# Routing of the sample tokens with two weight pieces kept in their buffers and a third buffer laid over keys and values

## The reference

```python
y = concat(attention_out, gdn_out) @ w_out              # mixer projection, 1024 x 1024
h = h + y
xb = rmsnorm(h, norm2)
q = (xb @ wq).reshape(-1, HP, 2, DPK // 2)              # HP = 8 heads; wq is 1024 x 2048
s = einsum('thcd,hcnd->thcn', q, keys)                  # 128 keys for each half of each head
s1, i1 = top_k(s[:, :, 0], 16);  s2, i2 = top_k(s[:, :, 1], 16)
cand = s1[..., :, None] + s2[..., None, :]              # 256 sums, of which the best 16
e = ...                                                 # number of an expert, 16384 in all
gate = softmax(sc);  hid = einsum('td,thkd->thk', xb, u[e])
h = h + einsum('thk,thkd->td', gate * gelu(hid), v[e])
```

## Time and profile before

| | |
|---|---|
| median of 3 runs | 2113.99 us |
| the profiled execution | 2111.61 us, span 2109.9 us |
| PE, DVE, ACT, POOL busy | 81%, 63%, 38%, 37% of the span |
| bytes moved | 779.61 MB; 369 GB/s over the span |
| chain that ended last | PE 36%, DMA 32%, DVE 16%, ACT 7% |
| L948, gathers | 576 issues |
| L782, loads of `w_route` | 20 issues of 2304 KB |
| L780, loads of `w_mixer` | 10 issues of 2048 KB |

### The profile page before, as it was taken

How to read it: one execution, slowest core, us unless ns; L and a number is a source line. 1 busy time by engine, 2 the same in 40 slices (tenths; PEclk the granted TensorE clock), 3 DMA queues, 4 the chain that set the end, 5 groups by cost and what they waited for, 6 DMA issues and landing times.

```text
span 2109.9 us, 20560 instructions
## 1 busy us (share of the span) xinstructions
PE 1713.4 (81%) x6211; PEld 863.1 (41%) x6211; DVE 1333.7 (63%) x3023; ACT 801.0 (38%) x2371; POOL 778.8 (37%) x704
## 2 busy tenths in 40 slices
PE   5889799988897878889797879978895567776877
PEld 1333364547453445445344535443551223442211
DVE  1343514344797657887665888865787866669554
ACT  1342321231545523563533455453243332323433
POOL 3123010111344543436334444634433554444442
PEclk9889899999999999999898999999898879888999
DMA  9999633128899999999999999999999999999997
GB/s 331 325 348 340 223 116 112 48 100 325 354 426 415 427 428 428 426 419 413 426 407 427 427 426 403 419 414 426 427 426 411 427 428 427 428 426 427 427 427 318
DMA packets 137479, 779.61 MB, mean 369 GB/s; under 512 B 14863, under 2 KB 23839, under 8 KB 59784
## 3 DMA queue, kind: packets, MB, share of 16 engines
q0 software_dynamic: 88384, 621.30, 70.6%
q1 hardware_dynamic: 45504, 149.69, 18.9%
q10 hardware_dynamic: 3480, 7.31, 0.9%
HBM read 762.27 MB, written 16.26 MB: 369 GB/s over the span
## 4 chain that ended last, share of the span: by engine, by line
PE 36%; DMA 32%; DVE 16%; ACT 7%; issue 4%; POOL 2%; SPq 1%; POOLq 1%; ACTq 0%; another core or an unknown queue 0%; DVEq 0%
DMA sb_uv<-in_peer_uv,sb_eidx 28%; PE bank L2145 17%; DVE sb_uv L1742 7%; PE bank L1763 6%; PE bank L2112 3%; PE bank L2080 2%; DMA sb_hres<-pre_conv 1%; ACT sb_diag L1321 1%; DVE sb_hres L1716 1%; POOL sb_uv L948 1%; ACT sb_ew L1314 1%; ACT L1310 1%; PE bank L1877 1%; PE bank L1889 1%; DVE sb_top L1643 1%
## 5 line engine op out<-in xcount | busy, mean ns | idle before, releaser
L2145 PE MATMUL bank<-sb_uv,sb_diag 128*128 128x512 f32 (+1 forms) x1860 | 960.1, 653 | 308.5 <-ACT sb_diag L1321 296.5
L948 POOL DMA_INDIRECT sb_uv<-in_peer_uv,sb_eidx x576 | 685.0, 1189 | 903.1 <-PE bank L2145 695.4
L1742 DVE CUSTOM_DVE_ANT_0 sb_uv<-sb_uv,sb_xn 128x1024 f32<-128x1024 f32 x576 | 698.9, 1221 | 326.2 <-DMA sb_uv<-in_peer_uv,sb_eidx 316.4
L2145 PEld LDWEIGHTS bank<-sb_uv,sb_diag 128*128 128x128 f32 (+1 forms) x1860 | 338.5, 197 | 806.2 <-ACT sb_diag L1321 470.2
L1310 ACT ACTIVATE sb_gel<-sb_h 128x1 f32<-128x1 f32 x576 | 116.3, 202 | 796.4 <-DVE sb_h L1742 790.0
L1763 PE MATMUL bank<-sb_w,sb_xnT 128*128 128x512 f32 (+1 forms) x560 | 270.9, 626 | 32.7 <-DMA sb_w<-in_w_sections 19.8
L1321 ACT ACTIVATE sb_diag<-sb_stay,sb_ew 128x128 f32<-128x128 f32 (+1 forms) x465 | 183.2, 394 | 48.5 <-PE bank L2145 5.3
L1314 ACT ACTIVATE sb_ew<-sb_gel,sb_gate 128x1 f32<-128x1 f32 x576 | 169.7, 295 | 19.8
L2112 PEld LDWEIGHTS bank<-sb_rT,sb_zone 128*128 128x128 f32 x1280 | 156.8, 196 | 28.3 <-issue 28.3
L1763 PEld LDWEIGHTS bank<-sb_w,sb_xnT 128*128 128x128 f32 (+1 forms) x560 | 99.5, 189 | 157.3 <-issue 121.9
L2112 PE MATMUL bank<-sb_rT,sb_zone 128*128 128x128 f32 x1280 | 157.8, 279 | 1.8 <-issue 1.8
(11 more groups left out here) (335 smaller groups left out, 1518.0 us busy)
## 6 DMA issues: line engine op xcount, KB each, us to landing
sb_zone<-in_w_route SPq DMA_DIRECT2D x20, 2304.0 KB
sb_w<-in_w_sections SPq DMA_DIRECT2D x40, 512.0 KB, 8.7
sb_zone<-in_w_mixer SPq DMA_DIRECT2D x10, 2048.0 KB
sb_uv<-in_peer_uv,sb_eidx POOLq DMA_INDIRECT x576
sb_sS<-in_cache_kT SPq DMA_DIRECT2D x32, 256.0 KB, 4.5
sb_zone<-in_cache_v POOLq DMA_DIRECT2D x32, 256.0 KB, 5.9
sb_zone<-in_cache_kT SPq DMA_DIRECT2D x32, 256.0 KB, 3.7
sb_hres<-pre_conv SPq DMA_DIRECT2D x6, 1024.0 KB
```

The lines of the kernel that those rows point to most:

```text
L948: nc.gpsimd.indirect_dma_start(uv[:, m % RING, :], None, i["peer_uv"], bass.IndirectOffsetOnAxis(ap=eidx[:, t % 2, n:n + 1], axis=0)).then ...
L1742: nc.vector.tensor_tensor_reduce(out=uv[:, m % RING, 0:D], in0=uv[:, m % RING, 0:D], in1=xn2[:, t % 2, :], scale=1.0, scalar=0.0, op0=ALU. ...
L2145: ins = nc.tensor.matmul(bank[half][0:rows, :], lhsT=G["diag"][:, d % DIAGS, 0:rows], rhs=uv[:, m % RING, D + 512 * half:D + 512 * half + ...
```

## The change

Three things change, all of them in the routing of tile 4 (and in the place of two tensors).

1. `kT` and `vtok` become two parts of one tensor, `attended`, with the same columns as before. Its first 4608 columns serve tile 4's routing as a third weight buffer.
2. Tile 3 leaves `w_route[2]` in the first buffer of `zone` and `w_route[3]` in the second. Tile 4 uses these two pieces where they lie, as its first two quarters: `turn_of` lets piece 2 go first, then 3, 0 and 1. Four loads stay: both mixer pieces and `w_route[0]` go one after the other into the buffer over keys and values, and `w_route[1]` into the first buffer of `zone`. They have a function of their own, `last_route_loads`, and `route_loads` is called for tiles 0 to 3 only.
3. The due slots of tile 4's routing: 384 + 46 + 1.05 k up to k = 4.9, and 8 more from there. The transposes and the first mixer half so come 20 slots earlier than before and all the rest 12 slots earlier; 8 more slots lie between the two halves. `choose_at` is as it was.

```diff
 def route_at(n, k):
-    return SLOTS * (n - 1) + (74 if n < PT else 66) + 1.05 * k
+    return SLOTS * (n - 1) + (74 + 1.05 * k if n < PT else 46 + 1.05 * k + (8 if k >= 4.9 else 0))
...
-        kT = keep("kT", [128, NH, TOK])
-        vtok = keep("vtok", [128, NT, HW])
+        attended = keep("attended", [128, NH * TOK + NT * HW])
+        kT = attended[:, 0:NH * TOK].rearrange("p (h r) -> p h r", h=NH)
+        vtok = attended[:, NH * TOK:].rearrange("p (t n) -> p t n", t=NT)
...
+        def route_part(n, part):
+            if n == PT and part in (0, 1, 2):
+                return attended[:, 0:ZONE]
+            return R["zone"][:, part % 2 if n < PT or part > 3 else 0, :]
+        def turn_of(n, g):
+            return (g + 2) % 4 if n == PT else g
...
+                def last_route_loads():
+                    yield route_at(PT, -8)
+                    sp.wait_ge(s_pv, NH * PT)
+                    sp.wait_ge(s_vst, 16 * (NT + 1))
+                    sp.dma_start(weights_part(PT, 0), i["w_mixer"][0].rearrange("p (k n) -> p k n", k=KC)).then_inc(s_wrl, 16)
+                    yield route_at(PT, 4)
+                    sp.wait_ge(s_yp, 2 * PT + 1)
+                    sp.dma_start(weights_part(PT, 1), i["w_mixer"][1].rearrange("p (k n) -> p k n", k=KC)).then_inc(s_wrl, 16)
+                    yield route_at(PT, 8)
+                    sp.wait_ge(s_yp, 2 * PT + 2)
+                    sp.dma_start(route_part(PT, 2), i["w_route"][0]).then_inc(s_wrl, 16)
+                    yield route_at(PT, 23)
+                    sp.wait_ge(s_s2p, 4 * PT + 1)
+                    sp.dma_start(route_part(PT, 3), i["w_route"][1]).then_inc(s_wr[0], 16)
...
                 def queries(n, g):
-                    m = 4 * n + g
+                    j = turn_of(n, g)
+                    m = 4 * n + j
...
                         if s == 0:
-                            pe.wait_ge(s_wr[g % 2], 16 * (3 * n + 2 + g // 2))
+                            if n < PT:
+                                pe.wait_ge(s_wr[g % 2], 16 * (3 * n + 2 + g // 2))
+                            elif g == 0:
+                                pe.wait_ge(s_wrl, 48)
+                            elif g == 1:
+                                pe.wait_ge(s_wr[0], 16 * (3 * PT + 1))
```

More of the change, by code:

```diff
@@ L572, in hybrid_step @@
         s_wr = [sem(f"route_weights_loaded{r}") for r in range(2)]
+        s_wrl = sem("route_weights_over_keys_loaded")
         s_g2 = sem("gain2_loaded")
@@ L767, in route_loads @@
                     for part in range(6):
-                        yield route_at(n, (-18 if n < PT else -4, -17 if n < PT else -3, 4, 7, 24, 32)[part])
-                        if part < 2 and n < PT:
+                        yield route_at(n, (-18, -17, 4, 7, 24, 32)[part])
+                        if part < 2:
                             sp.wait_ge(s_ob, 2 * (n + 2))
@@ L827, in _ @@
                 work += [Stream(q_spill(t)) for t in range(1, PT)] + [Stream(gdn_loads(u)) for u in range(NT)] + [Stream(query_load(n)) for n in range(1, PT)]
-                work += [Stream(route_loads(n)) for n in range(NT)] + [Stream(residual_load(n)) for n in range(NT)] + [Stream(past_biases())]
+                work += [Stream(route_loads(n)) for n in range(PT)] + [Stream(last_route_loads())] + [Stream(residual_load(n)) for n in range(NT)] + [Stream(past_biases())]
                 work += [Stream(key_loads(p)) for p in range(NPAIR)] + [Stream(store(t)) for t in range(NT)]
@@ L2076, in mix @@
                             if part == 0:
-                                pe.wait_ge(s_wr[half], 16 * (3 * n + 1))
+                                if n < PT:
+                                    pe.wait_ge(s_wr[half], 16 * (3 * n + 1))
+                                else:
+                                    pe.wait_ge(s_wrl, 16 * (half + 1))
                                 pe.wait_ge(s_mxc, 2 * (n + 1))
                             for k in range(4 * part, 4 * part + 4):
-                                ins = nc.tensor.matmul(bank[6 + half][:, :], lhsT=R["rT"][:, k, :], rhs=weights_half(half)[:, k, :], start=k == 0, stop=k == KC - 1)
+                                ins = nc.tensor.matmul(bank[6 + half][:, :], lhsT=R["rT"][:, k, :], rhs=weights_part(n, half)[:, k, :], start=k == 0, stop=k == KC - 1)
                         ins.then_inc(s_yp, 1)
```

46 lines of the change are left out of this document (23 added, 23 removed).

## The result

The changed kernel took 2106.24 us (median of 7 runs, 2098.74 to 2111.85), the kernel before beside it 2118.49 us (7 runs, 2113.4 to 2126.24). The ratio is 0.9945, 95% interval 0.9929 to 0.9961: 11.6 us less, between 8 and 15. The forecast was 12.0 us less. The forecast's time, 2102.0 us, was counted from the 2113.99 us of three runs; the seven runs of before that stand here have a median 4.5 us higher, which is why the time lies 4.2 us over it although the difference fits.

The account below looks back on a forecast made before the run. The prediction took DMA bytes at 427 GB/s to bound the kernel; -11.05 for two loads, -1.0 for a smaller burst and 0 for the rest made -12.0 us, from 2113.99 to 2102.0 us, range 2097 to 2110.

Parts of the forecast that it names:

- What bounds: From 1660 to 2080 us the DMA runs at its best rate, 427 GB/s, so a MB costs 2.342 us.
- The test sum: Check of the DMA limit, 1660 to 1960 us: 113 gathers, four route loads, one output, 128.4 MB, 300.8 us for 300.
- Two loads go: Tile 4 no longer loads `w_route[2]` and `[3]`: 4.72 MB at 427 GB/s, -11.05 us.
- The smaller burst: SP's loads at 1596 us shrink from 5.24 to 3.15 MB; half the gain from closing the rate dip, -1.0 us.
- The hole: Rate dip to 342 and 295 GB/s at the end of SP's burst behind tile 2's output, 2.0 us lost.
- Routing moved forward: Tile 4's same routing instructions run earlier; TensorE's 75.7 us of work fits, 0 us, at most +3.
- The new waits: TensorE's waits for tile 4's weight pieces are free; the second mixer piece lands in 13.5 of 23.5 us; 0 us.
- the ring hides a stall of 12 to 14 us: Gathers in flight keep the DMA fed; it runs dry only when TensorE's stall outlasts 12 to 14 us.
- rival C: Slower: second mixer piece lands late in the single buffer over keys and values; gain gone from 49 us; chance 0.04.
- A: Rival: VectorE or TensorE takes over as limit, part of the gain lost; gain 4 to 8 us, chance 0.14.
- B: Rival: the removed bytes moved while everything waited for something else; no gain, time 2114 us, chance 0.08.
- D: Rival: each load also takes 2.5 us completion from the stream, and the dip closes; -18 us, 2096 us, chance 0.04.

Follow-up runs that it names:

- e1: Changed kernel with `w_route` pieces 2 and 3 (4.72 MB) loaded again into the buffers where they already lie; ratio 1.0009 to the kernel before.
- e2: Kernel before, with tile 4's loads of `w_route` pieces 2 and 3 left out (timing only); ratio 0.9951 to the kernel before.
- e4: Changed kernel with none of tile 4's weight loads, 8.91 MB fewer (timing only); ratio 0.9853 to the kernel before.
- e3: Changed kernel with the due slots of tile 4's routing 12 later, the queries at their old place; ratio 0.9938 to the kernel before.
- e5: Changed kernel without the 8 slots between the mixer halves, the first half 8 slots later; ratio 0.9965 to the kernel before.

## Why the prediction was right

*What bounds.* Right in the stage. A byte is time at 427 GB/s, and e1, e2 and e4 measured it: 9.0 to 10.5 us for the 4.72 MB put back, 20.0 to 21.5 for the 8.91 MB taken away. (The test sum took 113 gathers; POOL issued 112 and one other instruction, so it is 298.4 us for the 300.)

*Two loads go, -11.05 us.* Right, and it is the whole of the result: -11.6 us, interval -15 to -8.

*The smaller burst, -1.0 us.* Wrong in its mechanism. The hole stayed at 2.0 us; the loads of the sample tokens made it, which stood in the same three rows of SP's timeline and which I had counted only as bytes. The trace of before already spoke against my reading. The DMA engines were busy in the hole (share 1.03 and 1.01 in the earlier trace rows), which transfers that come to their end would not give. And within 40 us behind the mixer pair issued at 1364.84 us, and behind the tile outputs at 884.61 and 1239.22, no 4 us window is under 420 GB/s; in the slots' part only tile 4 has loads of 64 rows. That alone would not have named the cause: the same trace has dips where no such load is near, 377 GB/s from 940 and 349 from 1416 us, again at a share of 0.95 or more, and no run looked into them. The term was small enough to leave the sum right, and that is luck: it was to be half of a gain that did not come.

*Routing moved forward, 0.* Right: e3 puts it back without effect. (The last scores are due at slot 384 + 54 + 48.3 = 486.3, and stood at 498.3; the prediction has both 0.2 too high, and nothing hangs on it.) The times came as worked out, counted from tile 2's output: transposes 114.5 us behind it (forecast 117.3), last scores 269.7 (271.3), tile 3's output 340.9 (342.3).

*The new waits, 0.* Right for the change: the second mixer piece landed after 11.3 us (forecast 13.5) and 24 us were there. The forecast had 11.0 us for the bytes at 190 GB/s and 2.5 us of completion on top, which in the earlier trace rows was the whole landing of the shortest DMA; the measured landing leaves hardly any room for such a part beside the bytes. But the step under it, that the ring hides a stall of 12 to 14 us, failed in e5: of 9.55 us about 4 were hidden. The ring did hold its 13.4 us of transfers. What was wrong was to set TensorE's stall against it, and not POOL's pause, which was 17.05 us: the matmuls behind the wait come on top, and TensorE began them at half its clock. So rival C was priced too mildly: with about 4 us of a stall hidden instead of 13, it would by an estimate from e5's one trace have eaten the gain from a landing of 23.5 + 4 + 12 = 40 us, not 49.

*A, B and D.* A (a consumer takes over) fell with e4. B (no gain) fell with the time itself, whose interval ends at 0.9961. D (a fixed cost for each load comes back too) would have made 18 us in the stage; 501.4 and 502.9 leave 11.3 to 12.8, and e4's 8.91 MB gave no more than their bytes.

## What to carry to other kernels

Where the DMA rate stands at its ceiling in every window while all engines have idle time, count bytes before anything else: a weight piece that is left in its buffer for the next tile is worth its size over the rate, wherever it stood. Order and buffers may then be chosen for what they let you leave out, but a load that waits for the work just before its use needs a gap as long as its landing time under full traffic (here 11.3 us for 2.10 MB). Do not count on a ring of prefetched data to hide the rest: it has to cover the pause of the engine that issues the gathers (here 17.05 us), and that is longer than the stall that caused it (9.55 us). A low rate with busy DMA engines is another thing than a low rate with idle ones; read both columns. Compare profiles from the last common event, not from their start: here the early part moved the spans by 5.6 us.

## What the runs showed of the hardware

- Two loads of 64 rows of 4 KB into the two halves of the partitions cost about 2 us of the rate beside full gathers, in all 12 traces in which they stand (277 to 383 GB/s in the two lowest windows of 4 us, at a DMA busy share of 0.98 to 1.05); one load of 128 rows did not (lowest 413).
- SP's queue got nearly half of the 427 GB/s beside the gathers: alone in its queue a load of 2.10 MB landed after 11.3 us (186 GB/s), one of 2.36 MB after 12.3 us (192 GB/s). Between an output and the sample tokens the 2.10 MB took 15.3 us.
- TensorE's granted clock was 0.50 right after a stall of 9.55 us, and four matmuls of 128x512 (recorded as eight) took 6.71 us instead of 3.60 (e5).
- Eight buffers of gathers kept the rate at 412 GB/s or more for 13.4 us after POOL's last instruction (e5).
- The same early part, up to tile 2's output, ended between 1594.2 and 1602.8 us in 14 executions, whatever the kernel. In one of them a granted clock of 0.50 to 0.52 from 628 to 640 us, where another had 1.00, let the rate fall to 31 GB/s.
